# A four-layer transformer stack on one core: the output product of its first and last mixers as three rounded products

## The chip, the cores and the metric

The kernel runs on one core of one Trainium2 chip. The metric is the time of the whole program on the device, in microseconds (us). The matrix engine is TensorE (PE, with its weight loads PEld), the vector engine VectorE (DVE), the activation engine ScalarE (ACT), the general one GpSimd (POOL), and SyncE (SP) issues the weight transfers. Each engine works through its own queue in order, and waits on semaphores for the others.

## The reference, cut to what matters

256 tokens of width 1024 pass four layers (feed-forward, mixer, feed-forward each; the mixers are of the kinds A, B, C, A) and then a second block (a hybrid mixer and a mixture of experts). The change concerns the output product `o @ w_out` of mixer A, which is layers 0 and 3:

```python
def sliding_sink_attention(h, w_in, w_out, sinks, rel_table):
    B, S, _ = h.shape
    qw, kw = N_HEADS * HEAD_DIM, A_KV_HEADS * HEAD_DIM
    q, k, v = jnp.split(h @ w_in, [qw, qw + kw], axis=-1)
    ...
    o = banded_attention(q, k, v, rel_table, A_WINDOW, sinks)
    return o.reshape(B, S, -1) @ w_out          # (256 x 1024) @ (1024 x 1024), float32

def banded_attention(q, k, v, rel_table, window, sinks=None):
    ...
        s = jnp.einsum("bqgrd,bkgd->bgrqk", q_n, k_n).astype(jnp.float32) * scale + bias
        ok = in_band & (start - pad + kj >= 0)
        p = masked_softmax(s, ok, sink)
        o = jnp.einsum("bgrqk,bkgd->bqgrd", p.astype(v.dtype), v_n)
```

## The kernel before, in words

**Stages.** The program is one list of blocks: feed-forward, mixer A, feed-forward, feed-forward, mixer B, and so on, with each feed-forward of 11 weight pairs. Weights stream through a ring of three slots of 6 x 1024 float32 per partition (`stream_weights`, L735). SP refills a slot when its last reader has signalled. Mixer A has five fills (`mixer_layout`, L558): keys and values, two halves of the query weights, and two halves of `w_out`, four rows of 128 x 1024 each (c = 0 and c = 1). The first half of `w_out` goes into the slot of the key and value weights, the second into that of the first query half.

**Two forms of a float32 product.** The plain form is one float32 matmul for each 128 x 128 weight tile (the trace has two records for it). The rounded form splits both operands into a high part, rounded to the reduced format fp32r, and a low part (value minus high), and adds three fp32r products: high x high, high x low, low x high. The feed-forwards and all of mixer C use the rounded form, mixers A and B the plain form for their output. Rounding costs one copy on ACT (high) and one subtraction on DVE (low) for each piece; a weight piece is 128 x 2048.

**Mixer A.** It has eight units: unit u is a quad of heads (u // 2) for one half of the tokens (a = u % 2). Odd units see 256 keys and so have twice the scores of even ones. Each engine walks the same steps j = 0 to 9, written out by hand:

- PE (`pe_mixer`, L1613): the scores of unit j; the transposes of the probabilities of unit j - 2; in steps 0 to 4 one query projection each (sixteen matmul records of 128 x 256, called the filler below); in steps 6 to 9 one group of the output product (`output_first`: rows c = 0 for one half of the tokens and one half of the columns, four plain matmuls, eight records); then the product with the values for unit j - 2. The scores of unit j wait until DVE has read those of unit j - 1 out of PSUM. After step 9 come the four closing groups, c = 1, and each ends one quarter of the result; a group with a = 0 waits for the copied result of unit 6, one with a = 1 for unit 7. The first group of all (step 6) waits for the copied results of units 0 to 3.
- DVE (`dve_mixer`, L1899): the softmax denominators of unit j - 1 (`coefficients`: small operations, then the reciprocal, which releases POOL); scale, bias and row maximum of unit j (`biased`); the evacuation of the projection; the copy of the result of unit j - 2 from PSUM to SBUF (`copy_out`, L1984).
- ACT (`act_mixer`, L2081): the copy of the transposed probabilities of unit j - 2 (`copy_pT`), then the four exponentials of unit j (L2107, L2110 for the sinks).
- POOL (`pool_mixer`, L2205): probabilities times reciprocal for unit j, as soon as DVE has its coefficients. PE transposes the outcome two steps later.

After the mixer ACT and DVE round the first feed-forward weights (L1274, L1286), and ACT squares each quarter of the result (L1045) for the norm; PE keeps its clock up with spare matmuls (L1209) until the normed input is there.

**Mixer C** (`pe_split_mixer`, L1776) has the same eight units and steps, but with the rounded output (L1844 to L1846), its weight pieces rounded at L941 and L948, and its results split into high (ACT, L2178) and low (DVE, L2052). Pieces lie where no live data is (`rows_views`, L901): "tail" is the last third of the piece's own slot, the others are free areas.

## Time and profile before

| | us |
|---|---|
| median of three runs | 2662.26 |
| lowest, highest | 2662.16, 2665.86 |
| the profiled execution | 2662.52 |
| its span | 2660.7 |
| PE busy | 2609.0 (98%) |
| DVE busy | 1745.3 (66%) |
| ACT busy | 1293.1 (49%) |
| POOL busy | 241.9 (9%) |
| mean granted TensorE clock | 0.991 |

The span is the profiled stretch, and the execution's own time is 1.8 us more. Busy shares are averages over the whole program. "The chain of waits" is the chain of work that ended last, followed back from the last instruction. The two A mixers lie at about 217 to 305 us and 1757 to 1845 us of the span. The granted clock is given as a share of full speed: 1.00 is 2.4 GHz, 0.50 is 1.2 GHz.

### The profile page before, as it was taken

To read this page: it belongs to the slowest core of one execution; us is meant where nothing else is said; L and a number is where in the kernel's file an instruction comes from. 1 tells how busy PE (TensorE), PEld (TensorE's weight loads), DVE (VectorE), ACT (ScalarE), POOL (GpSimd) and SP (SyncE) were. 2 spreads that over 40 slices of the span, in tenths; PEclk is the share of its full clock that TensorE was granted. 3 is DMA by queue.
4 is the path that set the end of the run, shared out by engine and by line. 5 is a ranking of instruction groups with operands and counts; after the bars stand their busy time and mean duration, and the time that the engine had idled before them with its cause. 6 is when DMAs were issued, how large, how long until landed. Compare 5 with 4: busy or idle time off the path is not lost.

```text
span 2660.7 us, 37977 instructions
## 1 busy us (share of the span) xinstructions
PE 2609.0 (98%) x13576; PEld 2103.9 (79%) x13576; DVE 1745.3 (66%) x2589; ACT 1293.1 (49%) x2041; POOL 241.9 (9%) x364
## 2 busy tenths in 40 slices
PE   8999999999998999999999999999999999899999
PEld 7887688888874788888988888886888654688887
DVE  6764577777674777777567777745776542577776
ACT  5444454544544544545565454435443221466665
POOL 0001100100111100101110010012001001000000
PEclk9999999999998999999999999999999999999999
DMA  9542555454332555453355545434553222478885
GB/s 321 193 148 87 180 207 189 153 204 179 116 115 82 219 191 192 151 189 141 135 183 215 192 169 190 158 135 150 194 197 132 95 95 71 178 276 287 302 299 191
DMA packets 337248, 472.40 MB, mean 178 GB/s; under 512 B 15632, under 2 KB 275056, under 8 KB 337152
## 3 DMA queue, kind: packets, MB, share of 16 engines
q1 hardware_dynamic: 334464, 464.02, 48.9%
q0 software_dynamic: 2192, 6.94, 0.8%
q8 instruction: 58, 0.95, 0.1%
q14 instruction: 38, 0.31, 0.0%
q10 hardware_dynamic: 496, 0.17, 0.0%
HBM read 470.01 MB, written 1.10 MB: 177 GB/s over the span
## 4 chain that ended last, share of the span: by engine, by line
PE 90%; DVE 5%; ACT 2%; issue 1%; DMA 1%; POOL 0%; SPq 0%; DVEq 0%; ACTq 0%; POOLq 0%
PE psum_all L1456 22%; PE psum_all L1460 12%; PE psum_all L1508 6%; PE psum_all L1509 6%; PE psum_all L1510 6%; PE psum_all L1593 4%; PE psum_all L2455 4%; PE psum_all L1718 3%; PE psum_all L3396 3%; PE psum_all L3415 3%; PE psum_all L3392 3%; PE psum_all L3393 2%; PE psum_all L1635 2%; PE psum_all L3420 1%; PE psum_all L2577 1%
## 5 line engine op out<-in xcount | busy, mean ns | idle before, releaser
L1456 PE MATMUL psum_all<-hT_both,gu_hi 128*128 128x512 f32 x2688 | 670.8, 391 | 0.3 <-DVE gu_lo L1286 0.3
L1456 PEld LDWEIGHTS psum_all<-hT_both,gu_hi 128*128 128x128 f32 x2688 | 492.8, 188 | 95.5 <-DVE gu_lo L1286 0.6
L1286 DVE TENSOR_TENSOR gu_lo<-raw_ring,gu_hi 128x2048 fp32r<-128x2048 f32 x176 | 402.1, 2286 | 15.1 <-ACT gu_hi L1274 9.6
L1460 PEld LDWEIGHTS psum_all<-hT_both,gu_lo 128*128 128x128 f32 x2688 | 366.7, 190 | 26.2
L1460 PE MATMUL psum_all<-hT_both,gu_lo 128*128 128x256 f32 x2688 | 374.8, 282 | 0.0
L1274 ACT ACTIVATE gu_hi<-raw_ring 128x2048 fp32r (+1 forms) x175 | 334.1, 1912 | 16.5 <-DVE oT L1982 8.1
L1281 ACT ACTIVATE down_hi<-raw_ring 128x1024 fp32r (+1 forms) x240 | 250.7, 1057 | 137.7 <-PE psum_all L1510 107.5
L1293 DVE TENSOR_TENSOR down_lo<-raw_ring,down_hi 128x1024 fp32r<-128x1024 f32 x240 | 292.5, 1219 | 34.4 <-ACT down_hi L1281 34.4
L1508 PE MATMUL psum_all<-down_hi,hidden_hi 128*128 128x512 f32 x704 | 277.2, 394 | 5.0 <-DVE hidden_lo L1384 4.3
L1509 PE MATMUL psum_all<-down_lo,hidden_hi 128*128 128x512 f32 x704 | 275.9, 392 | 0.0
L1510 PE MATMUL psum_all<-down_hi,hidden_lo 128*128 128x512 f32 x704 | 274.0, 389 | 0.0
L1436 POOL TENSOR_TENSOR hidden_hi<-hidden,consts_sb 128x256 fp32r<-128x256 f32 x176 | 108.1, 614 | 1295.0 <-DVE hidden L1380 1275.7
L1314 ACT ACTIVATE silu_gate<-silu_gate 128x256 f32<-128x256 f32 x176 | 73.5, 418 | 241.5 <-DVE silu_gate L1373 241.4
L1312 ACT ACTIVATE cross_terms<-psum_all 128x256 f32<-128x256 f32 x176 | 67.3, 382 | 210.9 <-PE psum_all L1460 210.9
L1384 DVE TENSOR_TENSOR hidden_lo<-hidden,hidden_hi 128x256 fp32r<-128x256 f32 x176 | 74.9, 425 | 141.2 <-POOL hidden_hi L1436 141.2
L3246 DVE TENSOR_TENSOR e_gate_up_lo<-raw_ring,e_gate_up_hi 128x2048 fp32r<-128x2048 f32 x64 | 146.6, 2291 | 31.3 <-ACT e_gate_up_hi L3239 30.7
L1508 PEld LDWEIGHTS psum_all<-down_hi,hidden_hi 128*128 128x128 f32 x704 | 132.8, 189 | 31.5 <-issue 7.0
L1377 DVE TENSOR_TENSOR up_scaled<-psum_all,cross_terms 128x256 f32<-128x256 f32 x176 | 74.5, 423 | 125.5 <-ACT cross_terms L1316 125.5
L1510 PEld LDWEIGHTS psum_all<-down_hi,hidden_lo 128*128 128x128 f32 x704 | 132.2, 188 | 29.0
L1509 PEld LDWEIGHTS psum_all<-down_lo,hidden_hi 128*128 128x128 f32 x704 | 132.9, 189 | 21.0
L1375 DVE TENSOR_TENSOR silu_gate<-silu_gate,rstd_rows 128x256 f32<-128x256 f32 x176 | 74.9, 426 | 86.7 <-ACT silu_gate L1314 86.7
L1316 ACT ACTIVATE cross_terms<-psum_all 128x256 f32<-128x256 f32 x176 | 66.8, 380 | 131.0 <-PE psum_all L1460 131.0
(490 smaller groups left out, 4079.1 us busy)
## 6 DMA issues: line engine op xcount, KB each, us to landing
raw_ring<-in_ffn_w_in SPq DMA_DIRECT2D x174, 1024.0 KB, 7.1
raw_ring<-in_w SPq DMA_DIRECT2D x96, 1024.0 KB, 7.8
raw_ring<-in_ffn_w_out SPq DMA_DIRECT2D x88, 1024.0 KB, 9.1
raw_ring<-in_c_w_in SPq DMA_DIRECT2D x12, 768.0 KB, 5.2
raw_ring<-in_w_in SPq DMA_DIRECT2D x10, 768.0 KB, 6.3
gain<-in_norm_g POOLq DMA_DIRECT2D x12, 512.0 KB, 4.1
raw_ring<-in_a_w_in SPq DMA_DIRECT2D x8, 768.0 KB, 5.2
raw_ring<-in_b_w_in SPq DMA_DIRECT2D x8, 768.0 KB, 5.0
```

What stands on the lines that cost most here:

```text
L1274: K.nc.scalar.activation(K.gu_hi[:, t, :, :], raw_gu(K, slot, t), ACT.Copy).then_inc(K.sem.gu_hi, 1)
L1281: K.nc.scalar.activation(K.dn_hi[:, t, :], raw_dn(K, slot, t), ACT.Copy).then_inc(K.sem.dn_hi, 1)
L1286: K.nc.vector.tensor_tensor(K.gu_lo[:, t, :, :], raw_gu(K, slot, t), K.gu_hi[:, t, :, :].bitcast(F32), ALU.subtract).then_inc(K.sem.gu_lo, 1)
L1293: K.nc.vector.tensor_tensor(K.dn_lo[:, t, :], raw_dn(K, slot, t), K.dn_hi[:, t, :].bitcast(F32), ALU.subtract).then_inc(K.sem.dn_lo, 1)
L1436: nc.gpsimd.tensor_tensor(K.hid_hi[:, t, :], K.hid[:, t, :], K.one.to_broadcast([P, SEQ]), ALU.mult)\
L1456: nc.tensor.matmul(out, K.gu_hi[:, t, j, :], K.hT_both[:, k, :, :].rearrange("p c s -> p (c s)"), start=k == 0, stop=False)
L1460: return nc.tensor.matmul(out[:, 0:SEQ], K.gu_lo[:, t, j, :], K.hT_hi[:, k, :], start=False, stop=k == KT - 1)
L1508: nc.tensor.matmul(out, h_hi, d_hi, start=first, stop=False)
L1509: nc.tensor.matmul(out, h_hi, d_lo, start=False, stop=False)
L1510: ins = nc.tensor.matmul(out, h_lo, d_hi, start=False, stop=last)
L1593: return K.nc.tensor.matmul(K.psum[:, item_bank(q), 0:n], lhsT, rhs, start=k == 0 and part == 0, stop=k == KT - 1 and part == 2)
L3246: K.nc.vector.tensor_tensor(K.ge_lo[:, t, :, :, :].rearrange("p k g f -> p g k f"), raw_expert(K, b, n, t), K.ge_hi[:, t, :, :, :].rearran ...
```

## The change

Mixer A's output takes the rounded form that mixer C has. Both halves of `w_out` are rounded in four pieces (0 to 3, two for each half): the high parts on ACT in steps 0, 1, 7 and 8, ahead of that step's exponentials (step 8 has none), the low parts on DVE in steps 0, 1, 8 and 9, after `biased`. The copy of each unit's result by DVE becomes two operations: the high part on ACT, after the exponentials of the step in steps 2 to 4 and ahead of them from step 5 on, and then the low part on DVE, at the end of the step, which waits for the high one. PE's output groups become twelve fp32r matmuls instead of four float32 ones, and wait for the low weight pieces. Mixer C keeps its order; its semaphore values now count from 4 and 8 times its place among the rounded outputs. Mixer B is not touched.

```diff
--- before.py
+++ after.py
@@ -467,7 +467,7 @@
         third = at("w_hi_third", [P, 2 * D], start + 2 * piece, F32R)
         spare = at("w_hi_spare", [P, 2 * D], self.pad_at, F32R)
         small = at("w_hi_small", [P, KT * 48], start + 17920, F32R)
-        self.w_hi = {"C": dict(e0=second, e1=third, e3=first), "B": dict(e0=first, e1=spare, small=small)}
+        self.w_hi = {"A": dict(e0=second, e3=first), "C": dict(e0=second, e1=third, e3=first), "B": dict(e0=first, e1=spare, small=small)}
         self.oT_hi = halves("oT_hi", self.arena)
         self.oT_lo = halves("oT_lo", self.pad_at)
 
@@ -485,7 +485,7 @@
     def plan(self):
         ins = self.ins
         fill = tile = item = unit = sunit = outs = 0
-        split = used = folded = turned = mixers = posts = chunk = 0
+        split = used = folded = turned = mixers = posts = chunk = rounded_outputs = 0
         ev = {"act": 0, "dve": 0}
         self.fills = []
         for n, b in enumerate(self.blocks):
@@ -514,6 +514,9 @@
                 mixers += 1
                 b["attn"] = Attn(kind)
                 b["loads"], b["items"] = self.mixer_layout(b)
+                if rounds_output(b):
+                    b["ro"] = rounded_outputs
+                    rounded_outputs += 1
                 if splits(b):
                     b["f"] = folded
                     folded += 1
@@ -597,6 +600,9 @@
             b["need_qk"] = [(4,), (6,), (8,), (10,)]
             b["need_v"] = [[2, 3]] * 4
             b["wo_step"] = 6
+            b["wo_place"] = ["tail", "e0", "tail", "e3"]
+            b["rows_high"], b["rows_low"] = {0: [0], 1: [1], 7: [2], 8: [3]}, {0: [0], 1: [1], 8: [2], 9: [3]}
+            b["high_first"] = 5
             wo = ins["a_w_out"][b["j"]]
         elif kind == "B":
             w = ins["b_w_in"][0]
@@ -876,6 +882,11 @@
     return b is not None and b["kind"] in ("B", "C")
 
 
+def rounds_output(b):
+
+    return b["kind"] in ("A", "C")
+
+
 def high_low(K, b):
 
     return (K.hT_hi, K.hT_lo) if folds(b) else (K.mT_hi, K.mT_lo[b["kind"]])
@@ -935,7 +946,7 @@
     for j in range(3):
         act.wait_ge(K.sem_raw[j], landed)
     place = b["wo_place"][c]
-    if place != "tail":
+    if place != "tail" and b["chunks"]:
         users = [y["last"] for y in b["chunks"] if y["place"] == place] or [len(b["items"]) - 1]
         act.wait_ge(K.sem.proj, b["item0"] + users[-1] + 1)
     K.nc.scalar.activation(high, raw, ACT.Copy).then_inc(K.sem.wo_hi, 1)
@@ -944,7 +955,7 @@
 def dve_rows_low(K, dve, b, c):
 
     raw, high, low, _ = rows_views(K, b, c)
-    dve.wait_ge(K.sem.wo_hi, c + 1)
+    dve.wait_ge(K.sem.wo_hi, 4 * b["ro"] + c + 1)
     K.nc.vector.tensor_tensor(low, raw, high.bitcast(F32), ALU.subtract).then_inc(K.sem.wo_lo, 1)
 
 
@@ -1564,6 +1575,20 @@
     return 0 if q == 0 else 2 if q % 2 else 3
 
 
+def rounded_output(K, pe, b, c, a, half):
+
+    pe.wait_ge(K.sem.wo_lo, 4 * b["ro"] + 2 * (c + 1))
+    cols, tok, nc = slice(half * 512, (half + 1) * 512), slice(a * P, (a + 1) * P), K.nc
+    out = K.psum[:, 2 * a + half, :]
+    for r in range(4):
+        _, high, low, _ = rows_views(K, b, 2 * c + r // 2)
+        o_hi, o_lo = (o[:, 4 * c + r, tok] for o in (K.oT_hi, K.oT_lo))
+        nc.tensor.matmul(out, o_hi, high[:, r % 2, cols], start=4 * c + r == 0, stop=False)
+        nc.tensor.matmul(out, o_hi, low[:, r % 2, cols], start=False, stop=False)
+        ins = nc.tensor.matmul(out, o_lo, high[:, r % 2, cols], start=False, stop=4 * c + r == 7)
+    return ins
+
+
 class RoundedProducts:
 
 
@@ -1712,6 +1737,8 @@
         ins.then_inc(K.sem.oPV, 1)
 
     def output(c, a, half):
+        if rounds_output(b):
+            return rounded_output(K, pe, b, c, a, half)
         slot = wait_fill(b["wo_fill"] + c)
         w = K.raw[:, slot, 0:4 * D].rearrange("p (r n) -> p r n", r=4)
         for r in range(4):
@@ -1776,7 +1803,6 @@
 def pe_split_mixer(K, pe, b):
     nc, att, units, items = K.nc, b["attn"], b["units"], b["items"]
     U0, S0, Q0, turn = b["unit0"], b["sunit0"], b["out0"], b["t"]
-    oT_hi, oT_lo = K.oT_hi, K.oT_lo
     rounds = RoundedProducts(K, pe, b)
 
     def project(q):
@@ -1835,16 +1861,7 @@
         ins.then_inc(K.sem.oPV, 1)
 
     def output(c, a, half):
-        pe.wait_ge(K.sem.wo_lo, 2 * (c + 1))
-        cols = slice(half * 512, (half + 1) * 512)
-        for r in range(4):
-            _, high, low, _ = rows_views(K, b, 2 * c + r // 2)
-            o_hi, o_lo = (o[:, 4 * c + r, a * P:(a + 1) * P] for o in (oT_hi, oT_lo))
-            out = K.psum[:, 2 * a + half, :]
-            nc.tensor.matmul(out, o_hi, high[:, r % 2, cols], start=4 * c + r == 0, stop=False)
-            nc.tensor.matmul(out, o_hi, low[:, r % 2, cols], start=False, stop=False)
-            ins = nc.tensor.matmul(out, o_lo, high[:, r % 2, cols], start=False, stop=4 * c + r == 7)
-        return ins
+        return rounded_output(K, pe, b, c, a, half)
 
     first_half = [(1, 0), (1, 1), (0, 0), (0, 1)]
 
@@ -1889,6 +1906,28 @@
             output(1, a, half).then_inc(K.sem.y_done, 1)
 
 
+def result_in_psum(K, x):
+    return K.psum[:, 6 + x["u"] % 2, 0:2 * P].rearrange("p (t s) -> p t s", t=2)
+
+
+def result_of(oT, x):
+    return oT[:, 2 * x["quad"]:2 * x["quad"] + 2, x["a"] * P:(x["a"] + 1) * P]
+
+
+def act_result_high(K, act, b, x):
+
+    act.wait_ge(K.sem.oPV, b["unit0"] + x["u"] + 1)
+    K.nc.scalar.activation(result_of(K.oT_hi, x), result_in_psum(K, x), ACT.Copy).then_inc(K.sem.oT_high, 1)
+
+
+def dve_result_low(K, dve, b, x):
+
+    dve.wait_ge(K.sem.oPV, b["unit0"] + x["u"] + 1)
+    dve.wait_ge(K.sem.oT_high, 8 * b["ro"] + x["u"] + 1)
+    K.nc.vector.tensor_tensor(result_of(K.oT_lo, x), result_in_psum(K, x), result_of(K.oT_hi, x).bitcast(F32),
+                              ALU.subtract).then_inc(K.sem.oT_sb, 1)
+
+
 def dve_query_scale(K, dve, b):
 
     dve.wait_ge(K.sem.r_pre, NT * (b["n"] + 1))
@@ -1998,11 +2037,15 @@
             coefficients(units[j - 1])
         if j < len(units) and units[j]["si"] is not None:
             biased(units[j])
+        for c in b["rows_low"].get(j, ()) if rounds_output(b) else ():
+            dve_rows_low(K, dve, b, c)
         for q in b["steps"][j] if j < len(b["steps"]) else ():
             evacuate_turned(q)
         if kind == "B":
             dve_compress(K, dve, b, j - b["cmp_step"])
-        if j >= behind:
+        if j >= behind and rounds_output(b):
+            dve_result_low(K, dve, b, units[j - behind])
+        elif j >= behind:
             copy_out(units[j - behind])
 
 
@@ -2041,16 +2084,6 @@
         d, co = K.den[:, i % RINGS, :], K.coef[:, i % RINGS, :]
         K.link(dve, "dve", nc.vector.tensor_scalar(d, d, TINY, None, ALU.max))
         nc.vector.reciprocal(co, d).then_inc(K.sem.coef, 1)
-
-    def quad_of(oT, x):
-        return oT[:, 2 * x["quad"]:2 * x["quad"] + 2, x["a"] * P:(x["a"] + 1) * P]
-
-    def copy_out(x):
-        dve.wait_ge(K.sem.oPV, U0 + x["u"] + 1)
-        src = K.psum[:, 6 + x["u"] % 2, 0:2 * P].rearrange("p (t s) -> p t s", t=2)
-        dve.wait_ge(K.sem.oT_high, x["u"] + 1)
-        nc.vector.tensor_tensor(quad_of(K.oT_lo, x), src, quad_of(K.oT_hi, x).bitcast(F32), ALU.subtract)\
-            .then_inc(K.sem.oT_sb, 1)
 
     dve_chunk_low(K, dve, b, 2)
     dve_query_scale(K, dve, b)
@@ -2075,7 +2108,7 @@
         for c in b["rows_in_step"].get(j, ()):
             dve_rows_low(K, dve, b, c)
         if j >= behind:
-            copy_out(units[j - behind])
+            dve_result_low(K, dve, b, units[j - behind])
 
 
 def act_mixer(K, act, b):
@@ -2127,12 +2160,18 @@
     for j in range(len(units) + 2):
         if j >= 2:
             copy_pT(units[j - 2])
+        for c in b["rows_high"].get(j, ()) if rounds_output(b) else ():
+            act_rows_high(K, act, b, c)
+        if rounds_output(b) and j >= b["high_first"]:
+            act_result_high(K, act, b, units[j - 2])
         if j < len(units) and units[j]["si"] is not None:
             exps(units[j])
         for q in b["steps"][j] if j < len(b["steps"]) else ():
             evacuate_tokens(q)
         if kind == "B":
             act_compress(K, act, b, j - b["cmp_step"])
+        if rounds_output(b) and 2 <= j < b["high_first"]:
+            act_result_high(K, act, b, units[j - 2])
     act.wait_ge(K.sem.oT_sb, b["outs"])
 
 
@@ -2169,13 +2208,6 @@
             act.wait_ge(K.sem.oPV, U0 + u - 1)
         nj = x["nk"] // P
         nc.scalar.activation(K.PT[:, u % 2, 0:nj, :], K.psum[:, 4:4 + nj, :], ACT.Copy).then_inc(K.sem.pT_sb, 1)
-
-    def out_high(x):
-        u, a = x["u"], x["a"]
-        dst = K.oT_hi[:, 2 * x["quad"]:2 * x["quad"] + 2, a * P:(a + 1) * P]
-        act.wait_ge(K.sem.oPV, U0 + u + 1)
-        src = K.psum[:, 6 + u % 2, 0:2 * P].rearrange("p (t s) -> p t s", t=2)
-        nc.scalar.activation(dst, src, ACT.Copy).then_inc(K.sem.oT_high, 1)
 
     for q in range(b["ahead"]):
         for c in b["high_at_item"].get(q, ()):
@@ -2196,7 +2228,7 @@
         for c in b["high_late"].get(j, ()):
             act_chunk_high(K, act, b, c)
         if j >= behind:
-            out_high(units[j - behind])
+            act_result_high(K, act, b, units[j - behind])
         for c in b["rows_in_step"].get(j, ()) if j >= len(units) else ():
             act_rows_high(K, act, b, c)
     act.wait_ge(K.sem.oT_sb, b["outs"])
```

## Rows read from the trace of the kernel before

**Rows 1.** The chain of waits in the first mixer A: start, duration, what.
```profile
267.34 1.03 ACT probsT L2122
270.74 3.44 PE psum_all L1718 x8
291.38 13.93 PE psum_all L1718 x32
```

**Rows 2.** The chain of waits at the end of mixer C.
```profile
1364.57 0.43 PE psum_all L1844
...
1375.68 2.16 PE psum_all L1209 x10
```

**Rows 3.** Instructions of mixer C's line L941: durations in ns, starts in us.
```profile
L941 ACT ACTIVATE raw_high<-raw_ring x2: 1904/1906/1907, 1334.4 to 1348.5; 128x2048 fp32r<-128x2048 f32 x2
```

**Rows 4.** Last transfer of the first `w_out` half, in each mixer A.
```profile
L839 SPq DMA_DIRECT2D raw_ring<-in_a_w_out x1: 432/432/432, 233.1 to 233.1; - x1
...
DMA to landing us min/median/max: 8.4/8.4/8.4
...
L839 SPq DMA_DIRECT2D raw_ring<-in_a_w_out x1: 432/432/432, 1772.8 to 1772.8; - x1
...
DMA to landing us min/median/max: 6.6/6.6/6.6
```

**Rows 5.** Timeline of DVE in the first mixer A: start, duration, operation, idle before.
```profile
239.87 0.69 DVE L1948 SCALAR_TENSOR_TENSOR scores_first<-psum_all,bias_full 128x512 f32<-128x512 f32 x1 [0.31 <-PE psum_all L1663]
...
254.67 0.16 DVE L1965 TENSOR_TENSOR attn_den<-attn_den,attn_sink_exp 128x4 f32<-128x4 f32 x1 [0.82 <-ACT attn_sink_exp L2110]
...
255.17 0.66 DVE L1942 SCALAR_TENSOR_TENSOR scores<-psum_all,bias_window 128x512 f32<-128x512 f32 x1
```

**Rows 6.** Timeline of ACT there: exponentials of units 0 and 3, first and last.
```profile
241.91 0.40 ACT L2107 ACTIVATE scores_first<-scores_first,attn_max 128x128 f32<-128x128 f32 x1 [8.02 <-DVE attn_max L1957]
...
243.47 0.19 ACT L2110 ACTIVATE attn_sink_exp<-attn_sink_exp 128x4 f32<-128x4 f32 x1
...
258.31 0.51 ACT L2107 ACTIVATE scores<-scores,attn_max 128x256 f32<-128x256 f32 x1 [1.79 <-DVE attn_max L1957]
...
260.30 0.19 ACT L2110 ACTIVATE attn_sink_exp<-attn_sink_exp 128x4 f32<-128x4 f32 x1
```

**Rows 7.** Timeline of mixer C: one result's high part (ACT) and low part (DVE).
```profile
1345.44 0.39 ACT L2178 ACTIVATE oT_hi<-psum_all 128x256 fp32r<-128x256 f32 x1
...
1345.93 0.42 DVE L2052 TENSOR_TENSOR oT_lo<-psum_all,oT_hi 128x256 fp32r<-128x256 f32 x1
```

**Rows 8.** Timelines of POOL and DVE, where one operation ends with the other's.
```profile
250.54 1.89 POOL L2211 TENSOR_TENSOR scores<-scores,attn_coef 128x1024 f32<-128x1024 f32 x1 [5.08 <-DVE attn_coef L1974]
...
296.27 2.15 POOL L1009 TENSOR_SCALAR stats<-stats 128x1 f32<-128x1 f32 x1 [11.38 <-ACT silu_gate L1045]
...
251.80 0.66 DVE L1954 TENSOR_TENSOR attn_max<-attn_max,sinks 128x4 f32<-128x4 f32 x1
...
293.84 4.49 DVE L1286 TENSOR_TENSOR gu_lo<-raw_ring,gu_hi 128x2048 fp32r<-128x2048 f32 x2 [1.98 <-ACT gu_hi L1274]
```

**Rows 9.** Timelines of DVE and POOL just after the reciprocal of unit 6.
```profile
276.98 0.68 DVE L1942 SCALAR_TENSOR_TENSOR scores<-psum_all,bias_window 128x512 f32<-128x512 f32 x1
...
277.14 1.04 POOL L2211 TENSOR_TENSOR scores_first<-scores_first,attn_coef 128x512 f32<-128x512 f32 x1 [2.89 <-DVE attn_coef L1974]
```

**Rows 10.** Stretches: length, busy us of PE, PEld, DVE, ACT, POOL, granted clock, DMA.
```profile
266.00:268.50 2.50, 1.39 (x14) 0.94 (x12) 2.31 (x4) 1.02 (x1) 1.04 (x1) 1.00 0.96 313
...
2280.00:2283.00 3.00, 0.47 (x4) 0.31 (x3) 2.57 (x3) 0.00 (x0) 2.21 (x1) 1.00 0.00 0
2283.00:2286.50 3.50, 3.50 (x11) 2.87 (x11) 2.79 (x16) 0.00 (x0) 0.00 (x0) 0.51 0.00 0
...
2310.40:2317.20 6.80, 6.80 (x24) 5.83 (x24) 1.80 (x3) 0.47 (x1) 0.00 (x0) 0.50 0.17 69
```

**Rows 11.** Timeline of ACT in the feed-forward after the first mixer A.
```profile
319.76 1.91 ACT L1274 ACTIVATE gu_hi<-raw_ring 128x2048 fp32r<-128x2048 f32 x1
```

## The prediction

> **What bounds the kernel now.** I read the busy table first: PE is busy for 98% of the span, so work taken from PE should be time, unless something else is late. Then the chain of waits through the first mixer A. It runs on PE almost everywhere; the one exception is ACT's copy of unit 3's transposed probabilities at 267.34 [rows 1], which PE waits for in step 5, where no projection fills the time. From there on the four output groups of steps 6 to 9 (3.44 us each) and the four closing ones (13.93 us, so 3.48 each, ending at 305.31) hold the chain. The timelines of DVE, ACT and POOL show what stands behind PE, and how much slack it has. The second mixer A repeats all of it 1539.7 us later.
>
> **What PE saves.** The plain group is 3.44 to 3.48 us [rows 1]. The rounded group is in this trace too: mixer C's four closing groups run from 1364.57 to 1375.68, 11.11 us, 2.78 each [rows 2]. Eight groups in each mixer save about 0.69 each, 5.5 us, or 11 for both. That would be all of it if PE stayed the bound.
>
> **The loop that has to carry the additions.** Softmax goes round between DVE and ACT: coefficients of unit j-1, bias and maximum of unit j, exponentials of unit j, and round again. Coefficients take 0.5 us (254.67 to 255.17), bias and maximum 3.1 for an odd unit (255.17 to the exponentials' start at 258.31) and 2.0 for an even one (239.87 to 241.9) [rows 5, 6]; an even one gets 0.5 more where POOL is working on the odd unit before (below). Exponentials take 2.2 us odd (258.31 to 260.49) and 1.75 even (241.91 to 243.66) [rows 6]. So a pair of units costs the loop 0.5 + 3.1 + 2.2 + 0.5 + 2.5 + 1.75 = 10.6 us. In steps 0 to 4 PE waits for the loop nowhere, so with its fillers it is the slower of the two; but as soon as the filler ends, in step 5, it waits at once [rows 1]. The loop has about an us a pair to give, and three things are put into it.
>
> **Added ahead of the loop.** A high weight piece is 1.9 us on ACT [rows 3], a low one 2.25 to 2.3 on DVE (two of the same shape take 4.49) [rows 8].
> - Piece 0 needs the whole first half of w_out. Its last transfer is issued at 233.1 and lands 8.4 later, at 241.5; in the second mixer 1772.8 + 6.6 = 1779.4, which is 239.7 on the first one's clock [rows 4]. In the second mixer piece 0 is rounded by 241.6, before unit 0's maximum is ready at 241.9: free. In the first it runs 241.5 to 243.4, and unit 0's exponentials start 1.5 late.
> - Low pieces 0 and 1 stand on DVE ahead of the next coefficients: 4.6 us, of which some 2.5 fall where DVE waited for exponentials anyway. With the landing, the loop is 3.2 us late at unit 2's exponentials in the first mixer and about 2 in the second.
>
> **Moved into the loop.** In steps 2 to 4 DVE's low result must wait for ACT's high one, which comes after the exponentials. Before, the copy to SBUF was hidden under them. High part to end of low part is 0.9 us less overlap (1345.44 to 1346.35) [rows 7]; I take 0.8 for each of three steps, 2.4. From step 5 on the high part goes ahead and is mostly hidden.
>
> **The walk.** Placing each queue's instructions in order with these durations gives, for the first mixer: exponentials of units 2, 3, 4 end at 257.3, 263.9, 269.5. ACT can copy unit 3's transposes only then, so PE's product for unit 3 starts at 270.8 instead of 268.4 [rows 1], after 2.6 us of idle. The first output group waits for the low result of unit 3, at 274.3, and ends at 277.1 instead of 274.2. From here PE follows the loop: second group ends 282.5, third 286.9. Exponentials of unit 7 end at 286.8, its coefficients at 287.3.
>
> **Unit 7's scaling.** Low piece 2 stands on DVE right behind those coefficients, and POOL's scaling of unit 7's probabilities starts on them too. They want the same thing: POOL's operation on one column, issued while DVE subtracts two weight pieces (293.84 to 298.33), takes 2.15 us and ends at 298.42; the other way about, DVE's four-column operation, 0.16 us elsewhere [rows 5], takes 0.66 and ends with POOL's at 252.4 [rows 8]. DVE is first: its next operation starts 0.16 us ahead of POOL's on the same reciprocal [rows 9], and its high piece has been there for 3 us. So I let POOL wait 2.3 us and start at 289.6, end 291.5. PE, done with unit 6 at 287.9, stands until 291.55, then transposes (1.0), last early group (2.76), values (1.0): the closing groups start at 296.4, and end at 307.5 instead of 305.3. The first mixer loses 2.1 us. In the second the same walk with the earlier landing loses 0.6. Sum +2.7.
>
> The rows show only a tiny POOL operation blocked by this subtraction. The Trainium skill, "SBUF — State Buffer", section "Who interferes with whom", says that a VectorE instruction with two SBUF inputs excludes a GpSimd one that reads SBUF for its whole duration, and that issue order decides who waits. By that rule the sum stays +2.7; if nothing blocked there, it would be 4 us less.
>
> The bounds of this cost: if POOL went first, both mixers end 2.0 earlier (-1.3 in sum); if no low piece blocked or was blocked, 2.2 earlier (-1.8). If DVE kept POOL out over low piece 3 as well, 2.7 later in each (+8.1).
>
> **The clock.** Before, PE's longest idle in the mixer is 1.1 us and the clock stays at 2.4 GHz (1.00 in 266.0 to 268.5) [rows 10]. Where PE stands some 2.5 of 3 us, the clock then falls to 1.2 GHz (0.51) for 3.5 us; after a gap of 3 us it once stayed there for 6.8 [rows 10]. The new gap ahead of unit 7's transposes is 3.6 us. At half clock for 3.4 us PE loses 1.7 us, and it is the bound there. For each mixer I take one such stretch, 1.7, and 0.3 for the gap ahead of unit 3's product, which the loop mostly hides. Bounds: nothing, or two stretches, 3.4 a mixer.
>
> **What costs nothing.** The closing groups' timetable is mixer C's: weights rounded for the feed-forward, squares, gains and norm all fit behind 11.1 us there [rows 2]. SP's refill behind the fourth output group was issued before the closing groups, 291.4 [rows 1], and is now issued at 295.3; with 8.4 us to land it is there at 304, and it is first read well after the feed-forward's first weights, at 319.8 [rows 11]; if that cover went, it would be 1 to 5 us. Low piece 3 (to 293.8) is done before the closing groups. New semaphore bases and the areas used cost nothing.
>
> **Sum.** The profiled execution took 2662.5 us (span 2660.7 and 1.8 around it), 0.3 above the median of the runs. Walk +2.7, half clock +3.4, middle gaps +0.6: 2669.2.
>
> **The rivals.** A measurement of this kernel tells about 0.2%, 5.3 us, from no change.
> 1. *Forecast:* the loop falls behind PE, unit 7's scaling waits for low piece 2, and the clock falls once in each mixer. 2669.2, its own range 2667 to 2672. Chance 0.40.
> 2. *Late loop, full clock.* The same waits, but the gaps don't lower the clock. For it: in mixer A neighbouring work is dense, and the gap of 1.1 did nothing. Against it: a gap of 3.6. 2665.2. Chance 0.24.
> 3. *No block at unit 7.* POOL gets in first or the block isn't total; then the longest gap is about 1.5 us at the end, and the clock holds. 2662.5 - 1.8 = 2660.7. Against it: both rows of the block. Chance 0.17.
> 4. *PE stays the bound.* My loop is too slow on paper, and waits are hidden. The whole 11 us: 2651.5. For it: mixer C, with the same steps, shows no gap on PE. Against it: C has three fp32r products in its fillers and so longer steps, and no large piece between coefficients and scaling. Half of the 11 falls here too, so that over 5.3 is gained. Chance 0.09.
> 5. *Worse end.* DVE keeps POOL out over low piece 3 too, and half clock lasts two stretches: 2662.5 + 8.1 + 6.8 = 2677.4. It decides where low piece 3 is issued before POOL gets in. Chance 0.10.
>
> **Numbers.** Slower by over 0.2% are cases 1 and 5, 0.50; within it 2 and 3, 0.41; faster 4, 0.09. The range 2658 to 2676 leaves out most of 4 and of 5. The cases below 5.3 us of change hold as much as those above, so the forecast's own range is the one given in 1.
>
> **What would show it.** In the trace after: output groups of 2.8 us in steps 6 to 9; unit 0's exponentials 1.5 us late in the first mixer and on time in the second; PE idle of 2 to 3 us ahead of the product for unit 3, put down to ACT; POOL's scaling of unit 7 (1.89 us alone) starting late or lasting about 4; PE idle of over 3 us ahead of unit 7's transposes, and a granted clock of about 0.5 behind it. I am wrong if PE has no waits over 1 us in the mixers (case 4), or if POOL's operation is on time (case 3), or if the clock stays at 1.00 (case 2).

## The result, and the profile after

Before the change 2663.45 us (median of 14 runs, 2661.95 to 2668.23), after it 2668.41 us (14 runs, 2660.85 to 2676.17). The ratio is 1.0020, 95% interval 1.0012 to 1.0029: some 5 us slower, 3 to 8 by the interval. The profiled execution of the changed kernel took 2675.48 us with a span of 2673.3.

I measure a mixer from the first keep-clock matmul of its block (the spare matmuls that PE runs while it waits for the normed input) to that of the next block. The first mixer A went from 89.7 us to 93.1, the second from 89.7 to 91.5, together +5.3. The profile's other 7.3 us of span lie in stages whose code is the same, and experiment 10 is about them.

The chain of waits through the first mixer, after the change (start, duration, what). It answers to [rows 1], where PE held the chain almost throughout:

```profile
254.94 1.15 ACT scores_first L2140 x6
...
256.55 0.42 DVE oT_lo L1927
...
260.94 1.66 ACT scores L2140 x7
...
272.90 1.67 ACT scores L2140 x7
...
283.54 1.67 ACT scores L2140 x7
...
285.99 3.86 POOL scores L2243
289.99 1.94 PE psum_all L1707 x8
...
308.67 2.16 PE psum_all L1220 x10
```

Now exponentials (ACT, L2140) and bias and maximum (DVE) alternate in it, up to POOL's scaling of unit 7. PE takes over only at 289.99. Its own timeline there (start, duration, what, idle before and who ended it):

```profile
269.36 1.09 PE L1730 MATMUL psum_all<-probsT,v_tok 128*64 128x256 f32 x8 [2.14 <-ACT probsT L2155]
...
272.84 0.50 PE L1586 MATMUL psum_all<-raw_high,oT_hi 128*128 128x512 f32 x1 [0.79 <-DVE oT_lo L1927]
...
289.99 1.94 PE L1707 MATMUL psum_all<-consts_sb,scores 128*128 128x128 f32 x8 [3.50 <-POOL scores L2243]
```

The first gap stands ahead of unit 3's product, the second ahead of the first output group, the third ahead of unit 7's transposes. Why the last is so long is in the timelines of DVE and POOL at unit 7:

```profile
285.74 0.18 DVE L2013 RECIPROCAL attn_coef<-attn_den 128x4 f32<-128x4 f32 x1
285.83 2.26 DVE L959 TENSOR_TENSOR raw_low<-raw_ring,raw_high 128x2048 fp32r<-128x2048 f32 x1
...
288.34 3.65 DVE L959 TENSOR_TENSOR raw_low<-raw_ring,w_hi_first 128x2048 fp32r<-128x2048 f32 x1
```

```profile
285.99 3.85 POOL L2243 TENSOR_TENSOR scores<-scores,attn_coef 128x1024 f32<-128x1024 f32 x1 [4.82 <-DVE attn_coef L2013]
```

Low piece 2 follows the reciprocal at once and keeps its 2.26 us. The scaling, recorded from 0.16 us later, takes 3.85 instead of 1.89 [rows 8]; low piece 3 then takes 3.65 instead of 2.28. What the gap does to the clock is in these windows (from:to, length, busy time of PE, PEld, DVE, ACT, POOL, then the granted clock, DMA share, GB/s):

```profile
285.50:289.00 3.50, 0.80 (x5) 0.20 (x4) 3.43 (x5) 2.35 (x3) 3.01 (x1) 0.99 0.00 0
289.00:292.00 3.00, 2.01 (x9) 2.04 (x10) 2.99 (x1) 0.03 (x1) 0.84 (x1) 0.50 0.00 0
292.00:296.00 4.00, 4.00 (x11) 3.09 (x11) 0.00 (x0) 0.99 (x1) 0.00 (x0) 0.53 0.00 0
296.00:299.00 3.00, 3.00 (x18) 1.86 (x17) 0.42 (x1) 0.84 (x2) 0.00 (x0) 1.00 0.38 109
```

The clock is at 1.2 GHz from about 289 to 296, and the transposes take 1.94 us instead of 1.1, the output group behind them 4.6 instead of 2.8. In the first mixer that is 6.8 us at half clock; in the second the same gap of 3.5 us is followed by 3.4 us of it.

One thing I had not seen coming is on ACT at step 0 of the second mixer:

```profile
1784.83 1.91 ACT L952 ACTIVATE raw_high<-raw_ring 128x2048 fp32r<-128x2048 f32 x1 [7.41 <-DMA raw_ring<-in_a_w_out]
1786.76 1.28 ACT L2140 ACT_TABLE_LOAD   x1
```

The load of the exponential's table stands directly ahead of the first exponential. Before the change it stood there too, but ran at once, while ACT waited for the maximum; in the kernel before, second mixer:

```profile
1772.31 1.28 ACT L2107 ACT_TABLE_LOAD   x1
1781.61 0.40 ACT L2107 ACTIVATE scores_first<-scores_first,attn_max 128x128 f32<-128x128 f32 x1 [8.02 <-DVE attn_max L1957]
```

Now the wait for the weight's landing is ahead of it in ACT's queue, so it is exposed in both mixers.

### The profile page after: what moved, and what is told of

It is laid out like the page before. It is cut to its first block, busy times and chain, and to the rows that moved or that the text cites. A ratio compares the mean times of both kernels' runs of the same rounds, so it can differ in the third digit from the quotient of the medians.

```text
span 2673.3 us, 38161 instructions
## 1 busy us (share of the span) xinstructions
PE 2611.3 (98%) x13640; PEld 2124.6 (79%) x13640; DVE 1762.4 (66%) x2597; ACT 1311.7 (49%) x2065; POOL 246.7 (9%) x364
## 4 chain that ended last, share of the span: by engine, by line
PE 85%; DVE 8%; ACT 3%; issue 2%; DMA 1%; POOL 1%; SPq 0%; DVEq 0%; ACTq 0%; POOLq 0%
PE psum_all L1467 22%; PE psum_all L1471 12%; PE psum_all L1519 6%; PE psum_all L1520 6%; PE psum_all L1521 6%; PE psum_all L2487 4%; PE psum_all L1618 3%; PE psum_all L3428 3%; PE psum_all L3447 3%; PE psum_all L3424 3%; PE psum_all L3425 3%; PE psum_all L3452 1%; PE psum_all L1745 1%; PE psum_all L2609 1%; PE psum_all L2628 1%
## 5 line engine op out<-in xcount | busy, mean ns | idle before, releaser
L1386 DVE TENSOR_TENSOR silu_gate<-silu_gate,rstd_rows 128x256 f32<-128x256 f32 x176 | 74.9, 425 | 86.7 <-ACT silu_gate L1325 86.7
```

## The experiments

All are edits of the changed kernel, in both mixers A. Ratios are to the kernel before, run on the same chip, with 95% intervals; the kernel before differs by up to 2 us from chip to chip, so versions are better compared by their ratios than by their medians. The mixers are in us, first and second. "Unit 7" is when its first exponential starts, in us from the mixer's start.

| | mixers | unit 7 | median us | ratio |
|---|---|---|---|---|
| before | 89.7, 89.7 | 64.7, 64.7 | 2663.45 | 1 |
| before, again | 89.7, 89.7 | 64.7, 64.7 | 2662.38 (one run) | |
| changed | 93.1, 91.5 | 67.7, 67.3 | 2668.41 | 1.0020 (1.0012 to 1.0029) |
| changed, again | 91.4, 91.2 | 67.1, 67.0 | 2669.53 | 1.0018 (1.0008 to 1.0029) |
| 1 POOL first | 88.5, 88.6 | 67.8, 67.8 | 2662.12 | 0.9987 (0.9978 to 0.9996) |
| 2 table early | 91.9, 91.6 | 66.9, 67.4 | 2668.25 | 1.0017 (1.0007 to 1.0027) |
| 3 low results later | 89.3, 90.7 | 65.0, 66.4 | 2663.49 | 0.9996 (0.9987 to 1.0005) |
| 4 spare matmuls | 90.2, 90.0 | 67.6, 67.3 | 2666.17 | 1.0006 (0.9996 to 1.0015) |
| 5 group in the gap | 88.2, 88.6 | 67.1, 67.5 | 2663.32 | 0.9995 (0.9986 to 1.0005) |
| 6 edits 1, 2, 3, 5 | 85.8, 86.2 | 65.0, 65.4 | 2656.41 | 0.9959 (0.9945 to 0.9972) |
| 7 edits 1, 2, 3 | 86.1, 85.8 | 65.4, 65.0 | 2656.18 | 0.9965 (0.9952 to 0.9977) |
| 8 pieces 0, 1 later | 91.7, 90.9 | 66.7, 66.6 | 2669.38 | 1.0013 (1.0004 to 1.0023) |
| 8b all of 6 and 8 | 85.8, 85.8 | 65.0, 65.0 | 2657.91 | 0.9975 (0.9965 to 0.9985) |
| 9 edits 1, 3 | 86.7, 86.1 | 66.0, 65.3 | 2656.05 | 0.9966 (0.9954 to 0.9979) |

Two things vary between profiles of the very same mixer, and both have to be taken out before two versions are compared. One is when the first half of `w_out` has landed. ACT starts to round piece 0 between 24.2 and 25.0 us after the mixer's start in the four mixers of the changed kernel, and unit 7 moves with it one for one: it comes 42.73 to 42.78 us behind that start in all four. The spread is widest in experiment 3, where the two starts are 24.2 and 25.7 us into their mixers (which begin at 214.38 and 1751.88):

```profile
238.62 1.91 ACT L952 ACTIVATE raw_high<-raw_ring 128x2048 fp32r<-128x2048 f32 x1 [7.10 <-DMA raw_ring<-in_a_w_out]
```

```profile
1777.57 1.91 ACT L952 ACTIVATE raw_high<-raw_ring 128x2048 fp32r<-128x2048 f32 x1 [8.57 <-DMA raw_ring<-in_a_w_out]
```

The other is the half clock behind unit 7. From unit 7's first exponential to the mixer's end it is 25.0 us in the kernel before. In the changed kernel it is 24.2 with 3.4 us of half clock (three mixers) and 25.4 with 6.8 (one).

**1. POOL's scaling first.**

```diff
+        if kind == "A" and j == 8:
+            dve.wait_ge(K.sem.psc, S0 + 8)
         for c in b["rows_low"].get(j, ()) if rounds_output(b) else ():
             dve_rows_low(K, dve, b, c)
```

> VectorE waits, in both mixers, until GpSimd has scaled the last unit before it makes the low part of late weight piece 2. Theory (the port block and the clock that follows it are the loss): GpSimd's last scaling takes 1.9 us instead of 3.85, TensorE's gap before the last transposes shrinks from 3.5 us to about 1.5, the granted clock stays at 1.00 there, and each mixer (from its first keep-clock matmul to the next block's) takes about 88.5 us instead of 93.1 and 91.5, the whole about 2660.5. Rival (the block costs only its own time, the clock falls all the same): each mixer 2 us less, the whole about 2664.5. Rival (the two low parts, now 2 us later, hold up the closing groups instead): mixers stay above 91 us, the whole about 2668.

The mixers come out at 88.5 and 88.6, the whole at 2662.1. POOL's scaling of unit 7, DVE's low piece 2 behind it, and the windows of granted clock in this kernel:

```profile
286.64 1.89 POOL L2245 TENSOR_TENSOR scores<-scores,attn_coef 128x1024 f32<-128x1024 f32 x1 [4.83 <-DVE attn_coef L2013]
```

```profile
288.56 2.29 DVE L959 TENSOR_TENSOR raw_low<-raw_ring,raw_high 128x2048 fp32r<-128x2048 f32 x1 [2.01 <-POOL scores L2245]
```

```profile
270.00:274.00 4.00, 4.00 (x22) 2.65 (x23) 3.28 (x8) 1.27 (x4) 1.04 (x1) 0.57 1.07 404
286.00:290.00 4.00, 2.40 (x16) 1.50 (x15) 1.93 (x4) 2.71 (x4) 1.89 (x1) 1.00 0.00 0
```

Both durations are back to what each has alone: the two had been blocking each other. The clock stays full at unit 7, and the mixers end 20.7 us behind unit 7's first exponential instead of 24.2 or 25.4, so the theory holds and both rivals fall. This profile has 3.4 us of half clock behind the gap ahead of unit 3's product (2.15 us here) in each mixer, where a gap of 2.14 in the changed kernel's profile brought none. There it cost nothing: unit 7 comes 42.76 us behind the start of piece 0's rounding, as without it.

**2. The table early.**

```diff
+        if kind == "A" and j == 0:
+            nc.scalar.activation(K.se[:, 3, 0:1], K.cst[:, 0:1], ACT.Exp)
         for c in b["rows_high"].get(j, ()) if rounds_output(b) else ():
             act_rows_high(K, act, b, c)
```

> One exponential of one column on ScalarE ahead of the rounding of late weight piece 0, so that the 1.28 us load of the exponential's table runs while ScalarE waits for the piece to land. Theory (the table load is what made the second mixer's first exponentials late): exponentials of unit 0 start 1.3 us earlier in both mixers (about 242.3 and 1786.8), the table load no longer stands behind the rounding, and each mixer is shorter by about 1 us, the whole about 2666.5. Rival (the time is caught up in the loop, where TensorE and VectorE wait anyway): the first exponentials are earlier and the mixers unchanged, the whole 2668.4.

The table was loaded at 232.99, out of the way, and the first exponentials came at 242.29 instead of 243.62. The mixers took 91.9 and 91.6, with the same half clock at their ends as in the changed kernel's first profile (6.8 and 3.4 us); the median did not move. With the landing taken out the two agree: unit 7 comes 42.2 us behind the start of piece 0's rounding instead of 42.75. So 0.5 us of the table's 1.28 reaches the end of each mixer, half of what the theory said, and whole runs can't resolve it.

**3. The low results one step later.**

```diff
-        if j >= behind and rounds_output(b):
+        if kind == "A" and 2 <= j <= 4:
+            if j >= 3:
+                dve_result_low(K, dve, b, units[j - 3])
+        elif j >= behind and rounds_output(b):
+            if kind == "A" and j == 5:
+                dve_result_low(K, dve, b, units[2])
             dve_result_low(K, dve, b, units[j - behind])
```

> In steps 3 to 5 of the loop VectorE makes the low part of the result one step later (units 0 and 1 in steps 3 and 4, units 2 and 3 in step 5), so that it no longer waits for ScalarE's high part, which stands behind the exponentials there. Theory (these waits, 1.8, 2.3 and 1.8 us of VectorE's idle time, push the whole softmax chain by about 0.8 us a step): the waits are gone, the last exponentials end about 2 us earlier than in the changed kernel, each mixer is shorter by about 2 us, the whole about 2664.5. Rival (ScalarE's exponentials set the pace of these steps, VectorE's waits are slack): mixers unchanged within 0.5 us, the whole 2668.

DVE's low results of steps 3 and 4 don't wait any more. Unit 0's in the changed kernel, with its idle ahead, and then in this one, with none:

```profile
256.55 0.42 DVE L1927 TENSOR_TENSOR oT_lo<-psum_all,oT_hi 128x256 fp32r<-128x256 f32 x1 [1.82 <-ACT oT_hi L1920]
```

```profile
258.29 0.41 DVE L1927 TENSOR_TENSOR oT_lo<-psum_all,oT_hi 128x256 fp32r<-128x256 f32 x1
```

The first mixer is 2.1 us shorter than in the changed kernel's second profile (which has as much half clock, 3.4 us), the second only 0.5 to 0.8. But in that second mixer the weights landed 1.2 to 1.5 us later than in the changed kernel's. Counted from the start of piece 0's rounding, unit 7 comes after 40.8 and 40.7 us instead of 42.75: the theory's 2 us are there in both. By the ratios the whole is 6 us below the changed kernel.

**4. Spare matmuls in the gap.** Nothing is sped up here; PE is only kept busy.

```diff
+        if b["kind"] == "A" and j == 9:
+            keep_clock(K, 8, 4)
         if 2 <= j < len(units) + 2:
             transposes(units[j - 2])
```

> Eight spare matmuls of 0.38 us (3.0 us in all, into the bank that the transposes fill next) on TensorE ahead of the last transposes in both mixers, in the gap of 3.5 us; nothing else is touched, GpSimd stays blocked. Theory (the half clock after the gap is a loss of its own, 2.8 us in the first mixer and 1.2 us in the second): the clock stays at 1.00 there, the transposes take 1.1 us instead of 1.9 and the last first-half group 2.8 instead of 4.6, the last unit still comes at the same time, the mixers take about 90.3 and 90.3 us, the whole about 2664.5. Rival (the clock's fall is not tied to this gap): the mixers stay at 93.1 and 91.5, the whole 2668.4.

PE's timeline around the gap, and two windows:

```profile
285.90 3.72 PE L1220 MATMUL psum_all<-consts_sb 128*128 128x256 f32 x16
289.47 1.07 PE L1707 MATMUL psum_all<-consts_sb,scores 128*128 128x128 f32 x8
```

```profile
285.50:289.50 4.00, 4.00 (x21) 3.03 (x19) 4.00 (x3) 1.83 (x2) 3.83 (x1) 1.00 0.00 0
289.50:293.50 4.00, 4.00 (x24) 3.16 (x25) 1.98 (x1) 1.03 (x1) 0.00 (x0) 1.00 0.00 0
```

POOL is blocked as before, the gap is filled with nothing useful, and the clock stays at 2.4 GHz. (The trace records two matmuls for each of the eight; they took 3.7 us, not 3.0.) The mixers come out at 90.2 and 90.0, where 90.3 was expected of each. This separates the two terms. At full clock the mixer ends 22.7 us behind unit 7's first exponential. So 3.4 us of half clock cost 1.5 us (24.2), and 6.8 us cost 2.7 (25.4): 4.2 in the changed kernel's first profile, 3.1 in its second. The waits alone make the two mixers 0.8 longer than before in this profile; in the changed kernel's, by the same 22.7, it is 1.0 in the first and 0.1 in the second, by when the weights landed. By the ratios the whole gains 3.7 us.

**5. The last first-half group in the gap.**

```diff
+        if b["kind"] == "A" and j == 9:
+            output_first(done)
+            done += 1
         if 2 <= j < len(units) + 2:
             transposes(units[j - 2])
```

> In both mixers the last first-half output group (2.8 us) goes ahead of the last transposes on TensorE, into the gap of 3.5 us, instead of behind them; GpSimd stays blocked. Theory (the gap is work time lost, and its clock too): the group fills the gap, the clock stays at 1.00, the closing groups start about 4 us earlier in the first mixer (293.5 instead of 297.5) and 2.9 us earlier in the second, mixers about 89.1 and 88.6, the whole about 2661.5. Rival (the wait for the copy of the turned probabilities, about 1.3 us, now stands open behind the transposes and opens a new gap with its own half clock): mixers above 90 us, the whole about 2665.

PE's idle ahead of the last transposes and of the last product is now

```profile
289.94 1.06 PE L1707 MATMUL psum_all<-consts_sb,scores 128*128 128x128 f32 x8 [0.54 <-POOL scores L2246]
292.12 1.09 PE L1730 MATMUL psum_all<-probsT,v_tok 128*64 128x256 f32 x8 [1.11 <-ACT probsT L2158]
```

Both the theory's fill and the rival's new wait are there; the wait is 1.1 us and brought no half clock. The mixers are 88.2 and 88.6 (expected 89.1 and 88.6), and end 21.1 us behind unit 7's first exponential, 1.6 sooner than with spare matmuls. (The second mixer has 3.4 us of half clock behind a gap of 1.85 us ahead of unit 3's product, again without cost.)

**6. Edits 1, 2, 3 and 5 together.**

> The four edits together in both mixers: GpSimd's last scaling ahead of the late low parts, the exponential's table loaded ahead of the landing, low parts of the results one step later in steps 3 to 5, and the last first-half group ahead of the last transposes. Theory (the savings of the three-product groups, 5.5 us a mixer, were there all along and were paid back by these four waits): each mixer about 85 us instead of 89.6 before the change, the whole about 2655.5, ratio to the kernel before about 0.9965. Rival (each wait removed uncovers the next, the chain of exponentials from unit to unit sets the end): mixers about 88 us as with GpSimd first alone, the whole about 2661.5.

The mixers take 85.8 and 86.2, the whole 2656.4 at a ratio of 0.9959: the theory is within 1.2 us, its rival is out.

**7. Edits 1, 2 and 3.**

> Three of the four edits in both mixers: GpSimd's last scaling first, table loaded early, low results one step later; the last first-half group stays behind the last transposes. Theory (with GpSimd unblocked TensorE's gap there is about 1.5 us, of which the moved group would hide all and then wait 1.1 us for the copy of the turned probabilities): mixers about 86.5, only 0.5 us longer than with all four (85.8 and 86.2), the whole about 2657.5. Rival (the moved group is the main part of the gain of the four): mixers about 88.5, the whole about 2661.5.

The mixers take 86.1 and 85.8, the whole 2656.2. Behind unit 7's first exponential it is 20.7 to 20.8 us with the moved group and without, so it gives nothing here, and the rival falls.

**8. Pieces 0 and 1 one step later**, alone, and with all four edits (8b).

```diff
-            b["rows_high"], b["rows_low"] = {0: [0], 1: [1], ...}, {0: [0], 1: [1], ...}
+            b["rows_high"], b["rows_low"] = {1: [0], 2: [1], ...}, {1: [0], 2: [1], ...}
```

> The changed kernel with weight pieces 0 and 1 rounded one step later in both mixers (steps 1 and 2 instead of 0 and 1), so that the first exponentials no longer stand behind the landing of piece 0. Theory (landing and table load together held up the start of the chain of exponentials, the landing more than the table): exponentials of unit 0 start about 2.7 us earlier than in the changed kernel (near 241.0 instead of 243.6), those of unit 1 about 1.5 us earlier (247.5 instead of 249.0), each mixer shorter by 1 to 2 us, the whole about 2665.5. Rival (VectorE's low part of 2.3 us in the step sets it, and this only moves one step on): exponentials of unit 2 start no earlier than 254.0, the mixers within 0.5 us of 93.1 and 91.5, the whole 2668.

> All four edits and weight pieces 0 and 1 rounded one step later, in both mixers. Theory (the start of the chain of exponentials still costs about 1 us behind the landing): mixers 84.8 and 85.2 instead of 85.8 and 86.2, the whole about 2654.5, ratio to before about 0.9955. Rival (VectorE's low part only moves on): mixers 85.8 and 86.2 within 0.4, the whole 2656.5.

Alone, unit 0's exponentials start at 242.81 in the first mixer, 26.5 us into it and as early as before the change, because it is the maximum that they wait for; the 241.0 of the theory was too early. Unit 7 comes 0.3 to 1.1 us sooner than in the changed kernel's four mixers, at 66.7 and 66.6 in both: the landing no longer sets it. With all four edits (8b) the mixers are 85.8 and 85.8, where the rival had 85.8 and 86.2 and the theory 84.8 and 85.2, and the ratio is no better than without.

**9. Edits 1 and 3 alone.**

> Two edits in both mixers: GpSimd's last scaling first, and the low results one step later in steps 3 to 5; the table is loaded where the changed kernel loads it. Theory (these two are nearly the whole gain; the table's 1.28 us is mostly taken up by VectorE's own work in step 0, as exponentials of unit 1 came only 0.5 us earlier with the table moved): mixers 86.7 and 86.2, the whole about 2657.5. Rival (each edit alone gained less than the three together because the table still held the chain): mixers 87.5 and above, the whole 2659.5.

With 1 and 3 in, nothing else is worth anything that whole runs can tell: 9, 7 and 6 have mixers of 85.8 to 86.7 and medians of 2656.1 to 2656.4. In the profiles the early table is still worth the same 0.5 us a mixer where the landing sets the start. The two-edit version beats both kernels: 9 us below before, by its ratio (6 to 12 by the interval). The mixers explain 6.6 of these. Its chain of waits shows why it stops there:

```profile
260.06 1.66 ACT scores L2147 x7
...
270.70 1.67 ACT scores L2147 x7
...
281.35 1.67 ACT scores L2147 x7
...
283.81 1.90 POOL scores L2250
285.85 1.06 PE psum_all L1707 x8
```

The exponentials of units 3, 5 and 7 come 10.64 and 10.65 us apart: that is the loop between DVE and ACT at its own pace, the 10.6 us for a pair that the prediction worked out, with PE holding up neither. The mixers are 3.0 and 3.6 us shorter than before the change (3.9 in 8b). By this chain the rest of PE's 5.5 us would need a shorter loop, which no run here tries.

**10. Both kernels profiled again.**

> The kernel before, unaltered, profiled a second time. The profile of the changed kernel and those of its three variants so far have the granted clock at half for 6.8 us more (two stretches of 3.4 us) in the first long stage behind the second mixer, whose code is not touched; the first profile of before has not. Theory (where the clock falls in the stages behind depends on when they are entered, which the change shifts, and it is no property of the change): this second profile of the same kernel may have these two stretches too. Rival (the change brings them about each time): the second profile shows that stage as the first did, 243.7 us with half clock in one place alone, against 246.9 us in the changed kernel's family.

> The changed kernel, unaltered, profiled and timed a second time. Theory: the two mixers take 93 and 91.5 us again (the waits and the half clock behind them belong to the kernel), while the stages behind them, whose code is the same as before the change, come out nearer to the kernel before (B's mixer 186 to 188 us, the first long stage 242 to 247 us): the whole about 2668. Rival (half clock behind the last unit is chance): the mixers differ from the first profile by 1.7 us or more.

The first long stage behind the second mixer took 243.6 us in the first profile of before and 246.9 in that of after. In the first of the two lines below, of after, PE is at half clock although its record shows it busy throughout (products of only 16 columns); the second is about the same place in before:

```profile
2070.00:2074.00 4.00, 4.00 (x9) 1.70 (x9) 3.75 (x9) 0.78 (x2) 0.00 (x0) 0.59 0.62 178
```

```profile
2064.00:2068.00 4.00, 4.00 (x10) 1.71 (x9) 3.75 (x10) 0.80 (x2) 0.00 (x0) 1.00 0.85 263
```

Repeated, before took 245.2 there and after 242.4; with experiment 4 it was 241.9, with 1 and 3 it was 247.0. The stage swings by 5 us with the half-clock stretches that fall in it, either way (6.8 and 10.2 us of them in before's two profiles, 13.7 and 3.4 in after's): the rival falls. Outside the mixers the changed kernel's span is 7.3 us longer in the first pair of profiles and 1.3 us shorter in the second, so that excess does not come with the change each time. What two profiles of each can't exclude is a small mean effect. The second part did not hold in full: the first mixer had 3.4 us of half clock this time instead of 6.8 and took 91.4, so the rival's 1.7 us came true for it, 1.1 of it from the clock and 0.6 from an earlier landing. The block and the gap of 3.5 us were the same. Why the clock stays down for 3.4 us behind them one time and for 6.8 another is not shown.

## Why the prediction came out as it did

Forecast 2669.2 from the sum +6.7; the mixers show +5.3 in one profile and +3.2 in the other, the medians +5.0. The mechanism is the forecast one (late loop, POOL blocked at unit 7, half clock behind the gap), but that the total came within an us is partly luck. The walk was 1.7 to 2.6 us too large. The sum started from 2662.5, and the median of the kernel before is 2663.45 by all its runs. And the stages that the change does not touch differ by +7.3 and -1.3 us in the two pairs of profiles, more than the whole effect.

- **PE's saving, 0.69 a group: right.** Rounded groups last 2.8 us in the mixers, and PE is no longer the bound.
- **The loop's slack, "about an us a pair": too large.** In the kernel before the exponentials of units 2 and 4 (252.89 and 263.53) are 10.64 us apart, the loop's own pace already. From unit 0 to unit 7 it took 38.2 us, and 37.5 in experiment 9, where the loop alone sets the pace: 0.7 us of slack in all. The sum does not use this figure, the walk places the instructions one by one.
- **Landing, 1.5 us late in the first mixer, on time in the second: right for a wrong reason, and wrong.** The difference between the two mixers was that of one profile: the same transfer took 8.4 and 6.6 us there, and 6.7 and 7.1 in the second profile of the kernel before. In the changed kernel's first mixer it took 7.3 and would have cost 0.5 (the high piece ends at 242.3, the maximum is there at 241.8); the 1.28 us of the table load took the rest's place (unit 0 at 243.62, 1.7 late), and stood in the second mixer as well. This term was missing, and 0.5 us of it reached the end (experiment 2). The landing itself reaches the end in full.
- **Low pieces 0 and 1: mis-sized, the largest error in the walk.** I had unit 2's exponentials 3.2 us late; they start at 254.44 against 252.89, 1.55 late. The two low pieces on DVE, and unit 1's first exponential on ACT:

```profile
242.34 2.29 DVE L959 TENSOR_TENSOR raw_low<-raw_ring,raw_high 128x2048 fp32r<-128x2048 f32 x1 [0.54 <-ACT raw_high L952]
...
248.91 2.28 DVE L959 TENSOR_TENSOR raw_low<-raw_ring,w_hi_second 128x2048 fp32r<-128x2048 f32 x1
```

```profile
249.04 0.51 ACT L2140 ACTIVATE scores<-scores,attn_max 128x256 f32<-128x256 f32 x1 [1.87 <-DVE attn_max L1996]
```

  Each lies beside the exponentials of its own unit (and piece 0 beside the table load), which DVE must wait for anyway. Of 4.6 us I had hidden 2.5; practically all of it is. The prediction also gives this step in three ways that don't agree: 1.5 for the landing and 2.1 not hidden make 3.6, the text says 3.2, and the walk's 257.3 for the end of unit 2's exponentials is 2.6 behind the kernel before (measured: 256.2).
- **Low results in steps 2 to 4, 0.8 each: about right.** The lateness grows from 1.55 at unit 2 to 2.2, 2.9 and 3.0 at units 3, 4 and 5 (exponentials at 260.52, 266.39, 272.49 against 258.31, 263.53, 269.50), 1.45 in all instead of 2.4. ACT after the change, units 4 and 5, and below it before:

```profile
266.39 0.40 ACT L2140 ACTIVATE scores_first<-scores_first,attn_max 128x128 f32<-128x128 f32 x1 [2.96 <-DVE attn_max L1996]
...
272.49 0.51 ACT L2140 ACTIVATE scores<-scores,attn_max 128x256 f32<-128x256 f32 x1 [1.59 <-DVE attn_max L1996]
```

```profile
263.53 0.40 ACT L2107 ACTIVATE scores_first<-scores_first,attn_max 128x128 f32<-128x128 f32 x1 [1.72 <-DVE attn_max L1957]
...
269.50 0.51 ACT L2107 ACTIVATE scores<-scores,attn_max 128x256 f32<-128x256 f32 x1 [1.14 <-DVE attn_max L1957]
```

  Experiment 3 gets 2 us back in each mixer. Unit 3's product comes at 269.36 instead of the 270.8 forecast, after 2.14 us of idle (2.6 forecast), the first output group at 272.84 instead of 274.3: both 1.4 to 1.5 us early, mostly by the low pieces.
- **Unit 7: the block is right, and decides.** POOL's end comes 3.9 us behind the coefficients, where I had 4.2, and PE's gap is 3.5 where I had 3.6. It isn't a late start but a longer duration in the record. By the rule of the Trainium skill, "SBUF — State Buffer", section "Who interferes with whom", that a VectorE instruction with two SBUF inputs shuts GpSimd's reads out, and the earlier one goes first, the trace agrees: 3.85 against 1.89 us, and the second low piece pays in turn, 3.65 against 2.26. Experiment 1 removes both.
- **Walk +2.7: too large.** Without half clock it is +0.8 in experiment 4, and +1.0 and +0.1 in the changed kernel's two profiles. The prediction's own 307.5 against 305.3 is 2.2 for the first mixer, and not 2.1.
- **Clock +3.4: near; +0.6: nothing.** A stretch of 3.4 us cost 1.5, where I had 1.7, and one of 6.8 cost 2.7: 4.2 and 3.1 us in two profiles. The +0.6 was for the gap ahead of unit 3's product, and where the clock fell there (experiments 1 and 5) it cost nothing.

Rival 2 (late loop, full clock) is out by the clock rows, rival 3 (no block) by POOL's 3.85, rival 4 (PE the bound) by the chain of waits. Rival 5's half clock of 7 us came true in one of the changed kernel's four profiled mixers, its block over low piece 3 in none: there POOL got in and piece 3 was the one that waited.

## What to carry to other kernels

When a change speeds up the bound engine, look for the loop that runs just behind it: its period is in the timeline of before, and here it capped a saving of 5.5 us a mixer at 3 to 4. Don't issue a large two-input VectorE operation on the same event that releases GpSimd on the critical path; ordering the two by one wait was worth 3.5 to 4.6 us a mixer here, 1.9 for the block itself and the rest for the clock, and later work had room for it. Price a TensorE gap with the clock behind it: a gap of 3.5 us cost 1.5 to 2.7 us more in the matmuls behind it, and spare matmuls kept that from happening. And before two profiles are compared, take out what differs between two profiles of one kernel: here the landing of a transfer moved a mixer by up to 1.4 us, and hid that experiment 3 works in both mixers.

## What I had not expected of the hardware

The table load of 1.28 us on ScalarE stands right ahead of the first exponential. It was hidden in the kernel before, where that exponential was the next thing that ScalarE waited for, and exposed once the rounding, with its wait for the landing, was put ahead. And two profiles of one kernel differ by up to 4.5 us in a stage of 240 us, by half-clock stretches of about 3.4 us each that fall there or don't, also where TensorE's record shows no idle. A gap of about 2.15 us ahead of unit 3's product brought such a stretch in experiment 1 and none in the changed kernel. A total from one profile can't be compared at this level; the length of a stage can, once its half clock and its transfers are accounted for.
